# Leaving out TensorE's nine products of constants during the first loads of a two-block kernel

## Reference

```python
# first block
f = _swiglu(_rmsnorm(h, ffn1_pre_g), ffn1_w_gate, ffn1_w_up, ffn1_w_down)
h = h + 0.5 * _rmsnorm(f, ffn1_post_g)
m = _token_mixer(_rmsnorm(h, mix_pre_g), w_in, ..., w_o)
h = h + _rmsnorm(m, mix_post_g)
...
# second block
u = _rmsnorm_2(h, norm_mix) @ w_in_2
...
return _rmsnorm_2(h, norm_final)
```

## Time and profile before

| | |
|---|---|
| median of 3 runs | 1568.49 us |
| all runs | 1568.17, 1573.45, 1568.49 us |
| the profiled execution's own time | 1573.5 us |
| its span, first to last instruction | 1571.8 us |
| TensorE busy | 1555.9 us, 99% of the span |
| VectorE, ScalarE, GpSimd busy | 758.5, 598.0, 154.8 us |
| mean granted TensorE clock | 0.996 of 2.4 GHz |

### The profile page before, as it was taken

One profiled execution on the slowest core, in us unless ns is written; L12 is line 12 of the kernel. 1 busy time (PEld: TensorE's weight loads), 2 busy tenths in 40 slices (PEclk: granted clock), 3 DMA queues, 4 the chain that ended last, 5 costly groups with the idle time before them and its releaser, 6 DMA issues.

```text
span 1571.8 us, 19059 instructions
## 1 busy us (share of the span) xinstructions
PE 1555.9 (99%) x7782; PEld 1280.7 (81%) x7782; DVE 758.5 (48%) x1202; ACT 598.0 (38%) x962; POOL 154.8 (10%) x162
## 2 busy tenths in 40 slices
PE   9999999999999999999999999999999999999998
PEld 7888888888888888888888888888878877777887
DVE  6444224336546533444743323433746454667645
ACT  6233222336433332334532223322664341444435
POOL 1211001101013400110111000110102000001100
PEclk9999999999999999999999999999999999999999
DMA  5433333333332322323233333333225421221322
GB/s 171 125 94 95 103 98 94 94 98 90 94 88 87 95 82 89 96 94 102 87 94 100 102 94 94 95 104 96 81 81 128 104 56 42 54 55 45 116 82 94
DMA packets 123735, 145.12 MB, mean 92 GB/s; under 512 B 18776, under 2 KB 86496, under 8 KB 123648
## 3 DMA queue, kind: packets, MB, share of 16 engines
q1 hardware_dynamic: 122080, 138.56, 29.5%
q0 software_dynamic: 1568, 5.34, 1.4%
HBM read 141.78 MB, written 2.10 MB: 92 GB/s over the span
## 4 chain that ended last, share of the span: by engine, by line
PE 94%; DVE 2%; ACT 2%; DMA 1%; issue 1%; SPq 0%; ACTq 0%; DVEq 0%
PE G L58 86%; PE X L58 5%; PE X L61 2%; DMA raw<-in_w_in_dram 1%; ACT sq_t L64 1%; PE G L61 1%; DVE prb L76 0%; ACT whi L64 0%; DMA raw<-in_ffn_w_up_dram 0%; DVE xl L73 0%; DVE f L70 0%; ACT xh L64 0%; DVE wlo L70 0%; ACT prb L64 0%; DVE h L73 0%
## 5 line engine op out<-in xcount | busy, mean ns | idle before, releaser
L70 DVE TENSOR_TENSOR wlo<-raw,whi 128x1024 fp32r<-128x1024 f32 (+3 forms) x261 | 313.3, 1209 | 497.6 <-ACT whi L64 497.5
L58 PE MATMUL G<-xh,whi 128*128 128x512 f32 (+1 forms) x1168 | 457.3, 393 | 1.9 <-ACT xh L64 1.0
L58 PE MATMUL G<-xl,whi 128*128 128x512 f32 (+1 forms) x1168 | 451.2, 388 | 0.8 <-DVE xl L73 0.8
L58 PE MATMUL G<-xh,wlo 128*128 128x512 f32 (+1 forms) x1168 | 450.3, 387 | 0.0
L64 ACT ACTIVATE whi<-raw 128x1024 fp32r<-128x1024 f32 (+3 forms) x261 | 266.3, 1030 | 463.0 <-DMA raw<-in_ffn_w_up_dram 161.3
L58 PEld LDWEIGHTS G<-xl,whi 128*128 128x128 f32 x1168 | 219.9, 188 | 46.6 <-DVE xl L73 1.2
L58 PEld LDWEIGHTS G<-xh,whi 128*128 128x128 f32 x1168 | 219.7, 188 | 45.9 <-ACT whi L64 1.2
L58 PEld LDWEIGHTS G<-xh,wlo 128*128 128x128 f32 x1168 | 220.2, 189 | 42.5
L70 POOL TENSOR_TENSOR tmp_t<-tmp_t,act_t 128x512 f32<-128x512 f32 x52 | 72.7, 1399 | 613.6 <-DVE tmp_t L70 472.7
L58 PE MATMUL G<-whi,ah 128*128 128x512 f32 x320 | 124.6, 389 | 0.0
L58 PE MATMUL G<-whi,al 128*128 128x512 f32 x320 | 124.5, 389 | 0.0
(11 more groups left out here) (271 smaller groups left out, 1812.4 us busy)
## 6 DMA issues: line engine op xcount, KB each, us to landing
raw<-in_w_in_dram SPq DMA_DIRECT2D x55, 512.0 KB, 3.6
raw<-in_ffn_w_gate_dram SPq DMA_DIRECT2D x88, 256.0 KB, 2.8
raw<-in_ffn_w_up_dram SPq DMA_DIRECT2D x88, 256.0 KB, 3.1
raw<-in_ffn_w_down_dram SPq DMA_DIRECT2D x44, 512.0 KB, 3.7
raw<-in_w_in_dram SPq DMA_DIRECT2D x12, 384.0 KB, 3.6
raw<-in_w_out_a_dram SPq DMA_DIRECT2D x8, 512.0 KB, 3.7
raw<-in_w_out_b_dram SPq DMA_DIRECT2D x8, 512.0 KB, 3.7
raw<-in_w_o_dram SPq DMA_DIRECT2D x8, 512.0 KB, 3.7
```

Source lines behind the costliest of these rows:

```text
L58: return self.e.matmul(out, lhs, rhs, start=start, stop=stop) if self.e else Idle()
L70: return self.e.tensor_tensor(*a) if self.e else Idle()
```

## The change

The helper `fill` and its three calls in `tensor` are left out: two products before the transpose of the gain rows, four before the transposes of x tiles 0 and 1, three behind them. The waits, and all other engines' programs, stay as they are.

```diff
@@ -642,18 +642,11 @@
-            def fill(n):
-                for _ in range(n):
-                    pe.matmul(G[3][:, 0:128], ident[:, :], ident[:, :], True, True)
-
             pe.wait_ge(const, "ident")
-            fill(2)
             pe.wait_ge(g_in, "g")
             pe.transpose(X[2][:, 0:8], rows[0:8, :], ident[0:8, 0:8]).then_inc(*prep_mm.event("g"))
-            fill(4)
             turn(0)
             turn(1)
-            fill(3)
             hooks = pre_hooks("s0")
             hooks[0, "half"] = lambda: (turn(2), turn(3))
             hooks[2, "half"] = lambda: (turn(4), turn(5))
             hooks[4, 0] = lambda: (turn(6), turn(7))
```

## The result

| | before | changed |
|---|---|---|
| median of 22 runs each | 1569.72 us | 1573.41 us |
| lowest, highest | 1568.02, 1575.0 | 1570.24, 1577.2 |
| ratio of times, 95% interval | | 1.002 (1.0012 to 1.0029) |
| span of the profiled execution | 1571.8 us | 1569.2 us |

The changed kernel is slower by 0.2%, between 1.9 and 4.6 us by the interval. Its profiled execution is one of the quickest and has a shorter span than the one of before, so the two spans must not be subtracted: the profile is read for where time went, the timed runs for how much.

The account below looks back on a forecast made before the run. TensorE, busy 99% of the span, was taken to bound the kernel. Removal gains 0, slow transposes cost 0 and low-clock first products 1.8 us, so 1568.49 + 1.8 = 1570.3 us, range 1568.0 to 1576.0.

Parts of the forecast that it names:

- Removed instructions gain nothing: Head: x transposes wait for the DMA and first products for `xh`, so removing nine products (18 instructions) gains 0.
- The slow transposes are covered: Head: eight x transposes at the low clock, 0.22 us apiece, delay nothing TensorE needs; cost 0, at most 0.45 us.
- the 422 "throughout": Sign in the changed profile: the first x transposes, at about 4.95 us, take 422 ns throughout.
- Low clock at the first products, 1.8 us: From 7.83 us, 9 of the first twelve real products run at the low clock, each 0.20 us slower: 1.8 us.
- The distances from dense work to the rise: 3.6 and 4.2 us from two places in the trace; counted from 7.83, the clock rises between 11.4 and 12.0.
- The share lost at the low clock: Time lost per us of TensorE's products at the low clock: (0.425 - 0.228) / 0.425, given as 0.47 us.
- All of it reaches the end: Behind the head: the chain from 7.83 us is unbroken and later waits are relative to TensorE, so all 1.8 us shows.
- The sum: Whole kernel: median before of 1568.49 plus 1.8 gives 1570.3 us, 0.11% more.
- the forecast's own case: Whole kernel: the clock rises late in the head and the median is of the low kind; 1569.6 to 1572.4, chance 0.50.
- the rival of the later low stretches: Thin passages as at 1206.7 us: more executions have the later low-clock stretches, median 1575.6 us; chance 0.27.
- The rival of the early rise: Head: x transposes raise the clock near or soon after 7.83 us; loss 0 to 0.4 us, 1568.5 to 1568.9; chance 0.17.
- The rival of a clock that stays low through the head: Head: transposes between products reset the rise; low until 27.79 us loses 9.4 us, 1577.9; chance of over 0.5% slower 0.04.

Follow-up runs that it names:

- e2_few_columns: Kernel before with its nine products of the identity streaming 8 columns instead of 128; median 1572.78 us, ratio 1.0012 (1.0 to 1.0025).
- c2_cut_after: Changed kernel with every engine's program ended behind the first half of the first SwiGLU; four timed runs, 216.21 to 216.52 us.
- c1_cut_before: Kernel before with every engine's program ended behind the first half of the first SwiGLU, no other edit; five timed runs, 214.86 to 215.04 us.
- e6_later_wait: Kernel before with four more products of the identity in TensorE's longest wait, ended at 1208.9 us; median 1570.26 us, ratio 0.9994 (0.998 to 1.0008).
- c3_cut_18_transposes: Kernel before, ended behind the first half of the first SwiGLU, each product of the identity replaced by two transposes of it; 214.83 to 215.24 us.
- e8_shift: Kernel before with eight more products of the identity behind its first twelve real products; median 1571.58 us, ratio 1.0005 (0.9994 to 1.0017).
- e3_first_six: Kernel before without the last three of its nine products of the identity; median 1572.49 us, ratio 1.0011 (0.9999 to 1.0023).

## Why the prediction was right, point by point

- *Removed instructions gain nothing.* Right: the first product starts at 7.75 against 7.83, behind the load and `xh`, and x's transposes at 4.88 against 4.95, behind the DMA.
- *The slow transposes are covered.* Right: they take 1.97 instead of 1.19 us, and `xh` and the first product are not late. (The first took 475 ns, not the 422 "throughout".)
- *Low clock at the first products, 1.8 us.* The mechanism is right, shown by its profile and by e2_few_columns and c2_cut_after. The size was 2.16 to 2.23 us in the profile of the full kernel, where eleven products and not nine were slow, since the clock rose near 12.5 instead of at 11.4 to 12.0, and 1.5 us in the cut kernel. The distances from dense work to the rise that I took from the trace, 3.6 and 4.2 us, are single draws. It was 4.7 here, and with the very head of before the 3.6 us were 5.3 in c1_cut_before and 5.8 in e6_later_wait. (The share lost at the low clock, (0.425 - 0.228) / 0.425, is 0.46 and not 0.47, which changes nothing.)
- *All of it reaches the end.* Right: 2.16 us at the wait that ends at 29.95.
- *The sum.* 1570.3 us was forecast and 1573.41 measured, inside the range (1568.0 to 1576.0). But it is outside the 1569.6 to 1572.4 that the forecast's own case was given: it is inside the range because that was widened for the rival of the later low stretches, which is in part luck. Two things lie between. The median of before was 1569.72 over 22 runs, not 1568.49 over three, which is 1.2 us. And the change cost 3.7 us in the medians in place of 1.8.
- *The rival of the early rise* did not happen, although the clock can rise with nothing but transposes before it, as in c3_cut_18_transposes. With the eight transposes from 4.9 to 6.9 us and 0.9 us of waiting, the clock was still low at the first real products in both profiles (after, c2_cut_after).
- *The rival of the later low stretches.* That they come and go is shown, in kernels whose code at that place is the same (three in the profile of before, one in that of after) and in the mean granted clocks of repeats. That the change brings more of them is not shown: its profile has fewer, and its 22 runs have a mean granted clock of 0.9966 on average, where before has 0.9965 to 0.9973 on the three chips.
- *The rival of a clock that stays low through the head* did not happen; the longest rise seen, in e2_few_columns, came behind all twelve products.

What stays open is the rest of the loss: 3.7 us between the medians, of which the head explains 1.5 to 2.2. The interval of the ratio reaches down to 1.9 us, and at equal granted clock the kernels differ by 1.6 to 2.4, so that the head is probably all of it and the rest is how many later low stretches the runs happened to have. The granted clocks of the 22 runs of before in the first table are not on record, so this is probable and not shown. e8_shift speaks against a cost of the shift itself. Whether the rise in the full kernel is on average later than in the four timed runs of the cut one was not measured.

## What to carry to other kernels

Work that produces nothing can have a use: before deleting it from a wait, compare the durations of the same instruction ahead of it and behind it, since 421 against 275 ns is the whole story here. What it was worth is the number of real instructions that then run at the low clock, times the difference in pace; here it was 1.5 to 2.2 us for the start, 0.7% of the cut kernel of 215 us and 0.1% of the full one. To measure such a term, cut the kernel behind the place in question: repeats of the two cut kernels agreed within 0.2 and 0.3 us where those of the full kernel spread over 7, and four runs of the cut kernel told more than eleven of the full. Where the kernel can't be cut, compare runs that have the same mean granted clock. And do not take the moment of the rise from one trace: with one and the same head it lay between 5.2 and 7.4 us.

## What the runs showed of the hardware that was not expected

- The clock rose behind transposes alone (c3_cut_18_transposes: 421 ns before, 273 from about 5.5 us on, runs of 214.83 to 215.24 us against 214.86 to 215.04 with products). Behind 18 instructions of 8 columns, shown busy, it was low until all twelve products were through (e2_few_columns, one profile).
- The moment at which the clock rises differs between executions of the same head: among the transposes near 5.2 us in the full e3_first_six, near 11.2 us in the cut one.
- The mean granted clock of a timed run tells which repeats are long: 34 runs of before at 0.998 have a median of 1568.86 us, 15 at 0.995 have 1573.00.
- A passage in which TensorE is shown fully busy can still end in a low stretch. In the kernel before, 3.40 us, mostly of small products (24 of the 28 have results of 64x31), are followed by the stretch at 1322.7 of the earlier trace rows; windows as there:

```profile
1319.30:1322.70 3.40, 3.40 (x28) 3.00 (x27) 1.28 (x2) 0.17 (x1) 0.00 (x0) 1.00 0.00 0
```

- The granted clock reads 1.00 in the first microseconds of every profile while the durations show the low clock; there the durations decide.
